# Gated delta rule, second chunk: its gate rows loaded ahead of its keys, with the gates' load ahead of the inverse; banks of the gate rows' filler emptied earlier; last tile's sum and bank copy exchanged

## The chip, the cores and the metric

The kernel runs on one core of a Trainium2 chip. The metric is the device time of one execution in microseconds; the median of three runs is compared.

## What is computed

One step of a recurrent decoder with three token mixers, over 1024 prompt tokens and 8 x 4 sample tokens (1056 columns in all), D_MODEL 1024, four heads of 128, float32. Cut to what matters here:

```python
def mixer(xn, p, st):
    proj = jnp.einsum('btd,dc->btc', xn, p['w_in'])
    ...
    conv = jax.nn.silu(sum(buf[:, j:j + t_len] * cw[j] for j in range(CONV_W)))
    cq, ck, cv = jnp.split(conv, 3, axis=-1)
    beta = jax.nn.sigmoid(gd_b)
    logg = -jnp.exp(p['gd_A_log']) * jax.nn.softplus(gd_a + p['gd_dt_bias'])
    o_gd, S1_gd = gdn_scan(l2n(heads(cq)) * HEAD_DIM ** -0.5, l2n(heads(ck)), heads(cv), beta, logg, S0_gd)
    y_gd = unheads(head_rms(o_gd) * p['gd_norm_w']) * jax.nn.silu(gd_z)
    ...

# gdn_scan, one chunk
    G = jnp.cumsum(gc, -1)
    decay = jnp.exp(jnp.where(incl, G[..., :, None] - G[..., None, :], -jnp.inf))
    A = eye + jnp.where(strict, bc[..., :, None] * kk * decay, 0.0)
    sol = lax.linalg.triangular_solve(A, rhs, left_side=True, lower=True, unit_diagonal=True)
    ...

# behind the mixers
    x = x + mix
    hid = jnp.square(jax.nn.relu(rmsnorm(x, p['norm2_w']) @ p['w_up']))
    x = x + hid @ p['w_down']
    # and a last rmsnorm of x
```

## The kernel before, in words

Every weight product (`dense`, L432) is made in three products of a high and a low part of weights and activations: a tile of 128 output rows by 1056 columns is three groups of 352 columns, each a chain of 24 matmuls in one of two PSUM banks `D`. A group can start when its bank was emptied by ScalarE (`evac_proj` at L451, for the tiles of the convolution `evac_conv` at L507 to L511 into `u_in`). For each weight tile SyncE (SP) loads `w_raw` (512 KB), ScalarE makes `w_hi` (L406) and GpSimd (POOL) makes `w_lo` (L412). A stored tile goes out by a DMA that ScalarE issues (L458, `proj<-stage`); it counts on `stage_stored`.

Each engine runs its own program in order; semaphores join them. The small steps of a mixer stand between pieces of weight tiles: at each `slot()`, a `Filler` puts the next few pieces (thirds of a group) of its tiles on PE, and on ScalarE and POOL the work that belongs to them. How many pieces a slot takes is a table (`ROW_SLOTS`, `GD_SLOTS`). On ScalarE a bank copy of a slot is kept back until the next slot (`late`), save where a slot has over four pieces, or `slot.evacuate()` is called.

Three places matter here.

1. **Gate rows** (`rows`, from 45 to 75 us). The rows of the gates (36 partitions) are loaded, VectorE and ScalarE make running sums, maxima and exponentials of them, and PE turns pieces of them (L1503 to L1512). Beside it PE fills in with tiles 2 and 3.

2. **The delta rule's first chunks** (`gdn`, from 250 us). The eight prompt chunks of 128 tokens follow one another. SP loads for each the keys and queries (`d_qk`), values (`d_v`), four gate rows broadcast over the partitions (`d_bc`), the gates `z` (`d_z`), each 256 KB for one DMA, and from the buffer `td` the diagonal blocks of an inverse (`d_t`, `d_tt`, 16 KB each, eight of them). The inverse was made by POOL and VectorE before, and SP writes it out to `td` (`inverse_loads(3)`, L716). The loads for chunk n + 1 are issued during chunk n, and VectorE and ScalarE prepare that chunk's decay there (`gdn_ahead`, L1569 and L1580). `stored_all` waits until the stores of all tiles below a number have landed; for `GD0` = 17 these are `stage_stored[0]` for tiles 0, 14 and 16 and `stage_stored[1]` for 1 and 15. It guards the load of `d_z` for the first chunk, since the tiles 14 to 16 are the gates.

3. **The last tile** (`last_down`). In the last feed-forward product each group (g, d) of a tile's eight output rows d is added to `acc` by VectorE (L2826), squared by ScalarE (L2821), and the squares are added up by VectorE (L2833). PE sums over the partitions (L2789 and L2790), ScalarE makes the root (L2782, L2784), and VectorE scales (L2794) what SP stores.

Of the kernel before, what the change touches and what calls it, by code (L numbers as in the profile page):

```python
# [9 lines left out]
ALU = mybir.AluOpType  # L10
# [18 lines left out]
KT = D_MODEL // P  # L29
# [68 lines left out]
class Tile:  # L98
# [8 lines left out]
    @property  # L107
    def slot(self):
        return self.base % 2
# [15 lines left out]
def build(nc, xT, w_proj, w_half, w_full, par, con, rowpar, segrow, m0, conv0, st_ml, st_mn, st_gd, st_hg,  # L125
# [6 lines left out]
    with ExitStack() as ctx:  # L132
# [1237 lines left out]
        def rows(kind, eng, slot):  # L1370
# [16 lines left out]
            if kind == "dve":  # L1387
# [39 lines left out]
                slot()  # L1427

# [38 lines left out]
            if kind == "act":  # L1467
                eng.wait_ge(*rw_dve.after("bc"))
# [20 lines left out]
                slot()  # L1489
                eng.wait_ge(*rw_pe.after("tok"))  # L1490
# [6 lines left out]
            if kind == "pool":  # L1497
                for _ in range(4):
                    slot()
            if kind == "pe":  # L1500
                slot()
                eng.wait_ge(*rw_dve.after("loc"))
                eng.transpose(M[1][0:1, 0:RP], r_a[0:RP, 0, last:CH], ident[0:RP, 0:RP])  # L1503
                eng.transpose(M[1][0:1, RP:2 * RP], r_l[0:RP, last:CH], ident[0:RP, 0:RP]).then_inc(*rw_pe.step("ends"))
                slot()
                eng.wait_ge(*rw_dve.after("mp"))
                eng.transpose(M[2][0:RP, 0:1], r_c[0:1, 3 * RP:4 * RP], ident[0:1, 0:1]).then_inc(*rw_pe.step("prev"))
                slot()
                eng.wait_ge(*rw_dve.after("kd2"))
                eng.wait_ge(*rw_act.after("ex2"))  # L1510
                for q in range(5):
                    i = eng.transpose(M[0][:, q * (RP + H):(q + 1) * (RP + H)], r_tok[q], ident[0:RP + H, 0:RP + H])  # L1512
                i.then_inc(*rw_pe.step("tok"))
                slot()
# [83 lines left out]
        def gdn(kind, eng, n, slot, sample, with_next=False, between=None):  # L1598
# [59 lines left out]
            if kind == "sp":  # L1658
# [8 lines left out]
                if between != "rest":  # L1667
                    for k in range(2):
                        eng.dma_start(hn(B.qk, k * C4), pcols(GD_TILE + 4 * (1 - k), 4, col0, N)).then_inc(gx_in if sample else gd_in, 16)
# [12 lines left out]
                eng.dma_start(hn(B.v), pcols(GD_TILE + 8, 4, col0, N)).then_inc(gx_in if sample else gd_in, 16)  # L1682
                if n is not None or sample:
                    prefetch(eng, None if sample else n, (gd_dve, "ge"))
                    token_rows()
# [3 lines left out]

                if sample:  # L1690
                    gates()
                    eng.dma_start(flat_bh(d_Ss), of_state(st_gd)).then_inc(gxs_ld, 16)
                    return
                prefetch(eng, n, (gd_dve, "zs"))
                if n is not None:
                    gates()
                else:
                    inverse_loads(eng, 3)
                    eng.wait_ge(zeroed, 2)
# [6 lines left out]
                if n is None:  # L1706
                    stored_all(eng, GD0)
                    gates()
                else:
                    slot()  # L1710
# [590 lines left out]
        SCALED = {3: (0,), 4: (1, 2), 5: (3, 4), 6: (5, 6), 7: (7,)}  # L2301
# [470 lines left out]
        def last_down(kind, eng):  # L2772
# [27 lines left out]
            for g, d in GROUPS if kind != "pool" else ():  # L2800
# [23 lines left out]
                if kind == "dve":  # L2824
                    eng.wait_ge(groups_done, n + 1)
                    eng.tensor_tensor(acc[:, d, cols(g)], acc[:, d, cols(g)], bank, ALU.add).then_inc(bank_free[n % 2], 1)  # L2826
                    if d:
# [3 lines left out]
                        else:  # L2831
                            eng.wait_ge(*dve_.after(f"a{g}{d - 2}"))
                            eng.tensor_tensor(SUM3[:, cols(g)], SUM3[:, cols(g)], SQ3[(d - 1) % 2][:, cols(g)], ALU.add).then_inc(*dve_.step(f"a{g}{d - 1}"))  # L2833
                    for k in SCALED.get(d, ()) if g else ():
                        scale(g - 1, k)
# [20 lines left out]
        ROW_SLOTS, ML_SLOTS = [9, 2, 4, 3], [3, 3, 3, 3, 3, 3]  # L2856
# [110 lines left out]
        def _(sp):  # L2967
# [61 lines left out]
            chunk_loads(sp, gdn, LOOP_GD, 0, 3)  # L3029
# [255 lines left out]
```

## Time and profile before

| | |
|---|---|
| median of 3 runs | 2195.5 us (2195.11 to 2198.4) |
| the profiled execution | 2200.46 us |
| its span | 2198.7 us |
| busy: PE / VectorE / ScalarE / POOL | 99% / 44% / 34% / 26% |
| mean granted clock of TensorE | 0.995 |

The profiled execution is a run of its own; its time is 1.8 us above its span, which is the time outside of the first and the last instruction. All rows come from it. Times in rows are microseconds from the start of the span, unless marked ns.

### The profile page before, as it was taken

Reading aid. Unit: us, or ns where it says so; the run is one execution under the profiler, and the core shown is the slowest. Engines: PE = TensorE matmul, PEld = TensorE weight load, DVE = VectorE, ACT = ScalarE, POOL = GpSimd, SP = SyncE. Lnnn points to the kernel's source line nnn. Section 1 sums busy time; section 2 is a strip of 40 time slices with the busy share of each in tenths; the row PEclk is TensorE's granted clock in tenths of the full one; section 3 lists DMA queues with packets and bytes.
Section 4 is the critical chain, followed back from the end, with each engine's and each line's share of the span. In section 5 each row is a group of like instructions: output and inputs, shape, how many; then the busy total and the mean of one; then the engine's idle time right before and its main releaser. Section 6 shows DMA issues by size and latency. Waiting matters only on the chain.

```text
span 2198.7 us, 36263 instructions
## 1 busy us (share of the span) xinstructions
PE 2166.3 (99%) x13762; PEld 2104.9 (96%) x13762; DVE 971.9 (44%) x1522; ACT 758.2 (34%) x1342; POOL 571.2 (26%) x375
## 2 busy tenths in 40 slices
PE   7999999999999999999999999999999999999998
PEld 6999999999899999899998999999999999999997
DVE  5888323333665664244445365442222222222225
ACT  5556323232465563233332333231312213122132
POOL 2438623323211212212212222212221221212120
PEclk9999999999999999999999999999999999999999
DMA  4224536442244323456431744202111111111112
GB/s 173 67 80 135 162 114 188 128 133 89 83 125 144 99 97 118 128 161 193 143 109 59 254 148 146 97 25 58 29 58 34 52 52 33 57 33 52 52 40 88
DMA packets 191538, 222.09 MB, mean 101 GB/s; under 512 B 38670, under 2 KB 146226, under 8 KB 191334
## 3 DMA queue, kind: packets, MB, share of 16 engines
q1 hardware_dynamic: 164364, 179.81, 27.0%
q10 hardware_dynamic: 27098, 41.23, 5.3%
q8 instruction: 53, 0.87, 0.2%
q14 instruction: 23, 0.19, 0.0%
HBM read 162.22 MB, written 58.77 MB: 101 GB/s over the span
## 4 chain that ended last, share of the span: by engine, by line
PE 79%; issue 8%; POOL 4%; DVE 4%; DMA 2%; ACT 2%; SPq 1%; ACTq 0%; POOLq 0%; DVEq 0%
PE D L432 65%; PE D L2811 2%; POOL w_lo L412 2%; POOL b_t L738 1%; POOL b_u L735 1%; DVE u_x L546 1%; PE MM L1302 1%; PE MM L1890 1%; DMA proj<-stage 0%; PE MM L2367 0%; PE MB L1974 0%; PE MM L872 0%; PE MB L2284 0%; PE D L2367 0%; PE MB L2234 0%
## 5 line engine op out<-in xcount | busy, mean ns | idle before, releaser
L432 PE MATMUL D<-xn_hi,w_hi 128*128 128x352 f32 x1992 | 663.7, 333 | 7.3 <-ACT stage L451 2.8
L412 POOL TENSOR_TENSOR w_lo<-w_raw,w_hi 128x1024 fp32r<-128x1024 f32 (+1 forms) x163 | 338.7, 2078 | 1184.7 <-ACT w_hi L406 1184.7
L432 PE MATMUL D<-xn_lo,w_hi 128*128 128x352 f32 x1992 | 644.2, 323 | 0.0
L432 PE MATMUL D<-xn_hi,w_lo 128*128 128x352 f32 x1992 | 643.9, 323 | 0.0
L432 PEld LDWEIGHTS D<-xn_hi,w_hi 128*128 128x128 f32 x1992 | 375.7, 189 | 22.5 <-issue 12.8
L432 PEld LDWEIGHTS D<-xn_lo,w_hi 128*128 128x128 f32 x1992 | 375.8, 189 | 4.7 <-issue 3.8
L432 PEld LDWEIGHTS D<-xn_hi,w_lo 128*128 128x128 f32 x1992 | 375.5, 189 | 0.0
L406 ACT ACTIVATE w_hi<-w_raw 128x1024 fp32r<-128x1024 f32 (+1 forms) x163 | 143.7, 882 | 346.8 <-PE D L432 296.4
L432 PE MATMUL D<-z_lo,w_hi 128*128 128x352 f32 x768 | 247.9, 323 | 0.0
L432 PE MATMUL D<-z_hi,w_lo 128*128 128x352 f32 x768 | 247.8, 323 | 0.0
L432 PE MATMUL D<-z_hi,w_hi 128*128 128x352 f32 x768 | 247.2, 322 | 0.0
L432 PE MATMUL D<-h_lo,w_hi 128*128 128x352 f32 x672 | 217.1, 323 | 0.0
L432 PE MATMUL D<-h_hi,w_lo 128*128 128x352 f32 x672 | 216.6, 322 | 0.0
L432 PE MATMUL D<-h_hi,w_hi 128*128 128x352 f32 x672 | 216.5, 322 | 0.0
L2748 DVE TENSOR_TENSOR acc<-acc,D 128x352 f32<-128x352 f32 x168 | 87.5, 521 | 225.0 <-PE D L432 225.0
L451 ACT ACTIVATE stage<-D 128x352 f32<-128x352 f32 x177 | 80.8, 457 | 239.8 <-PE D L432 223.5
L432 PEld LDWEIGHTS D<-z_hi,w_hi 128*128 128x128 f32 x768 | 144.2, 188 | 0.1
L432 PEld LDWEIGHTS D<-z_hi,w_lo 128*128 128x128 f32 x768 | 144.3, 188 | 0.0
L432 PEld LDWEIGHTS D<-z_lo,w_hi 128*128 128x128 f32 x768 | 144.2, 188 | 0.1
L2734 ACT ACTIVATE f_v<-f_u 128x352 f32<-128x352 f32 x96 | 47.8, 498 | 246.2 <-DVE f_u L2741 246.2
L432 PEld LDWEIGHTS D<-h_hi,w_hi 128*128 128x128 f32 x672 | 126.3, 188 | 0.0
L432 PEld LDWEIGHTS D<-h_hi,w_lo 128*128 128x128 f32 x672 | 126.2, 188 | 0.0
(557 smaller groups left out, 3066.6 us busy)
## 6 DMA issues: line engine op xcount, KB each, us to landing
w_raw<-in_w_proj SPq DMA_DIRECT2D x73, 512.0 KB, 3.7
proj<-stage ACTq DMA_DIRECT2D x60, 528.0 KB, 3.3
w_raw<-in_w_half SPq DMA_DIRECT2D x72, 256.0 KB, 2.7
w_raw<-in_w_full SPq DMA_DIRECT2D x24, 512.0 KB, 3.6
stage<-proj SPq DMA_DIRECT2D x23, 528.0 KB, 3.6
d_bc<-rowd SPq DMA_DIRECT2D x32, 256.0 KB, 5.7
m_in<-proj SPq DMA_DIRECT2D x32, 256.0 KB, 3.8
f_w<-in_w_full SPq DMA_DIRECT2D x16, 512.0 KB, 3.5
```

The source lines that it names most:

```text
L406: nc.scalar.activation(w_hi[t.slot][:, 0:kt, :], buf[:, 0:kt * P].rearrange("p (k m) -> p k m", m=P), ACT.Copy).then_inc(w_hi_made, 1)
L412: nc.gpsimd.tensor_tensor(w_lo[t.slot][:, 0:kt, :], raw(t)[0][:, 0:kt * P].rearrange("p (k m) -> p k m", m=P), w_hi[t.slot][:, 0:kt, :].bi ...
L432: last = nc.tensor.matmul(D[b][:, 0:GN], w[t.slot][:, k, :], x, start=(k == 0 and n == 0), stop=(k == kt - 1 and n == 2))
L451: nc.scalar.activation(stage[:, t.slot, g * GN:(g + 1) * GN], D[t.bank(g)][:, 0:GN], ACT.Copy).then_inc(bank_free[t.bank(g)], 1)
L546: eng.scalar_tensor_tensor(x, conv_in(c)[:, j + 1:j + 1 + CONV_LEN], tap(j + 1), x, ALU.mult, ALU.add).then_inc(*cv_dve.step(f"{now}{c}"))
L735: pool.tensor_tensor(part, b_a[:, k + 1:BLK, k:k + 1].to_broadcast([P, n, k + 1]), b_t[:, k, 0:k + 1].unsqueeze(1).to_broadcast([P, n, k + ...
L738: pool.tensor_tensor(b_t[:, k + 1:BLK, 0:k + 1], b_t[:, k + 1:BLK, 0:k + 1], part, ALU.subtract).then_inc(*iv_pool.step(f"t{k}"))
L1302: i = eng.matmul(level(j, slice(0, N))[:, h * (N // 2):(h + 1) * (N // 2)], hn(g_kl, j * N4)[:, h, :], g_ql[:, j * HF + h * (N // 2):j * H ...
L1890: i = eng.matmul(MM[0:N, h * 2 * N:(h + 1) * 2 * N].rearrange("p (x n) -> p x n", n=N), hn(B.qk, C4)[:, h, :], q_and_k, start=True, stop=True)
L2734: eng.activation(v, u, ACT.Square).then_inc(f_sq, 1)
L2748: eng.tensor_tensor(acc[:, m - FT, cols], acc[:, m - FT, cols], D[t.bank(g)][:, 0:GN], ALU.add).then_inc(bank_free[t.bank(g)], 1)
L2811: last = eng.matmul(bank, w[:, k, :], x[:, k, cols(g)], start=(k == 0 and j == 0), stop=(k == FT - 1 and j == 2))
```

## The change

Four edits. In `rows`, the first slot of nine pieces is split in three and six, every engine gets one more slot, and ScalarE calls `slot.evacuate()` in two places. In `gdn` for SP, a new mode `ahead` issues only the waits and the four `d_bc` loads of the next chunk, and `behind` the rest; the second chunk's loads (n = 0) are taken out of the loop and written with them. In the same function, for the first chunk, `stored_all` and the load of `d_z` are placed ahead of `inverse_loads(3)`, where they stood behind the loads of `d_t` and `d_tt`. In `last_down`, for the last of the eight rows, VectorE's sum of squares stands ahead of the addition to `acc`, and the scaling of one piece goes from the seventh to the eighth step.

```diff
@@ rows, ScalarE and PE
             if kind == "act":
+                slot()
+                slot.evacuate()
                 eng.wait_ge(*rw_dve.after("bc"))
...
                 slot()
+                slot.evacuate()
                 eng.wait_ge(*rw_pe.after("tok"))
...
             if kind == "pe":
+                slot()
                 slot()
                 eng.wait_ge(*rw_dve.after("loc"))
@@ gdn, SP
                 if between != "rest":
-                    for k in range(2):
-                        eng.dma_start(hn(B.qk, k * C4), ...)
+                    if between != "ahead":
+                        for k in range(2):
+                            eng.dma_start(hn(B.qk, k * C4), ...)
...
-                eng.dma_start(hn(B.v), pcols(GD_TILE + 8, 4, col0, N))...
-                if n is not None or sample:
+                if between != "ahead":
+                    eng.dma_start(hn(B.v), pcols(GD_TILE + 8, 4, col0, N))...
+                if (n is not None or sample) and between != "behind":
                     prefetch(eng, None if sample else n, (gd_dve, "ge"))
                     token_rows()
...
+                if between == "ahead":
+                    return
...
                 if n is not None:
                     gates()
                 else:
+                    stored_all(eng, GD0)
+                    gates()
                     inverse_loads(eng, 3)
                     eng.wait_ge(zeroed, 2)
...
-                if n is None:
-                    stored_all(eng, GD0)
-                    gates()
-                else:
+                if n is not None:
                     slot()
@@ last_down, VectorE
-                    eng.wait_ge(groups_done, n + 1)
-                    eng.tensor_tensor(acc[:, d, cols(g)], acc[:, d, cols(g)], bank, ALU.add)...
+                    def gather():
+                        eng.wait_ge(groups_done, n + 1)
+                        eng.tensor_tensor(acc[:, d, cols(g)], acc[:, d, cols(g)], bank, ALU.add)...
+
+                    if d < KT - 1:
+                        gather()
                     if d:
...
+                    if d == KT - 1:
+                        gather()
@@ tables and the SP program
-        SCALED = {3: (0,), 4: (1, 2), 5: (3, 4), 6: (5, 6), 7: (7,)}
+        SCALED = {3: (0,), 4: (1, 2), 5: (3, 4), 6: (5,), 7: (6, 7)}
-        ROW_SLOTS, ML_SLOTS = [9, 2, 4, 3], [3, 3, 3, 3, 3, 3]
+        ROW_SLOTS, ML_SLOTS = [3, 6, 2, 4, 3], [3, 3, 3, 3, 3, 3]
...
-            chunk_loads(sp, gdn, LOOP_GD, 0, 3)
+            gdn("sp", sp, 0, None, False, between="ahead")
+            load_w(sp, Tile(LOOP_GD + 2), w_proj[LOOP_GD + 2])
+            gdn("sp", sp, 0, lambda: load_w(sp, Tile(LOOP_GD + 3), w_proj[LOOP_GD + 3]), False, between="behind")
+            chunk_loads(sp, gdn, LOOP_GD, 1, 3)
```

SP's queue around the first chunk, before: the rest of the first chunk's loads (from `d_v`) and the loop's first turn up to its first load. In a row stand the line, what the DMA writes and reads, its shape, and the semaphores that it waits for.

```order
50 L1682 DMA d_v<-proj 128x4x128 [waits cv_st0,rw_mo,cv_st1,rw_out,rw_dve,rw_act,rw_pe]
51 L716 DMA td<-b_t 128x1024 [waits iv_pool]
52 L716 DMA td<-b_tt 128x1024 [waits iv_dve]
53 L1705 DMA d_t<-td 32x4x32 [waits iv_st,zeroed]
54 L1705 DMA d_t<-td 32x4x32 x3
55 L1705 DMA d_tt<-td 32x4x32 [waits iv_stt]
56 L1705 DMA d_tt<-td 32x4x32 x3
57 L1688 DMA d_z<-proj 128x4x128 [waits stage_stored1,stage_stored0]
```

And now:

```order
50 L1689 DMA d_v<-proj 128x4x128 [waits cv_st0,rw_mo,cv_st1,rw_out,rw_dve,rw_act,rw_pe]
51 L1695 DMA d_z<-proj 128x4x128 [waits stage_stored1,stage_stored0]
52 L716 DMA td<-b_t 128x1024 [waits iv_pool]
53 L716 DMA td<-b_tt 128x1024 [waits iv_dve]
54 L1716 DMA d_t<-td 32x4x32 [waits iv_st,zeroed]
55 L1716 DMA d_t<-td 32x4x32 x3
56 L1716 DMA d_tt<-td 32x4x32 [waits iv_stt]
57 L1716 DMA d_tt<-td 32x4x32 x3
58 L1680 DMA d_bc<-rowd 128x4x128 [waits gd_dve,gd_pool,gd_pe]
59 L1680 DMA d_bc<-rowd 128x4x128 x3
60 L384 DMA w_raw<-in_w_proj 128x1024 [waits w_lo_made]
61 L1675 DMA d_qk<-proj 128x4x128 [waits gd_pool,gd_pe]
```

`d_z` with its wait for the stores went from behind the reads of the inverse to ahead of its writes; the four `d_bc` loads of the second chunk come before weight tile 19 and the keys.

ScalarE in the gate rows, before (`rw_dve`, `rw_act`, `rw_pe` count the steps of the rows, `groups_done` the groups of PE):

```order
53 L1469 ACTIVATE r_row<-r_a 36x256 [waits rw_dve]
54 L1471 ACTIVATE r_a<-r_row 36x256 [waits rw_act]
...
58 L1477 ACTIVATE r_row<-r_a 36x128 [waits rw_act]
59 L406 ACTIVATE w_hi<-w_raw 128x1024 [waits w_loaded1,groups_done]
60 L507 ACTIVATE u_in<-D 128x352 [waits groups_done] x2
...
69 L406 ACTIVATE w_hi<-w_raw 128x1024 [waits w_loaded0,groups_done]
70 L1493 ACTIVATE tok<-MB 128x4x8 [waits rw_pe]
71 L1493 ACTIVATE tok<-MB 128x4x8 x4
72 L1495 ACTIVATE tok<-MB 32x5x4
73 L507 ACTIVATE u_in<-D 128x352 [waits groups_done] x2
```

And now:

```order
53 L406 ACTIVATE w_hi<-w_raw 128x1024 [waits w_loaded1,groups_done]
54 L507 ACTIVATE u_in<-D 128x352 [waits groups_done]
55 L1472 ACTIVATE r_row<-r_a 36x256 [waits rw_dve]
...
60 L1480 ACTIVATE r_row<-r_a 36x128 [waits rw_act]
61 L507 ACTIVATE u_in<-D 128x352 [waits groups_done]
...
70 L406 ACTIVATE w_hi<-w_raw 128x1024 [waits w_loaded0,groups_done]
71 L507 ACTIVATE u_in<-D 128x352 [waits groups_done] x2
72 L1497 ACTIVATE tok<-MB 128x4x8 [waits rw_pe]
```

`w_hi` of tile 3 and the first bank copy of tile 2 went ahead of the first exponential, and two bank copies of tile 3 ahead of the `tok` copies.

## Rows read from the trace of the kernel before

**Rows 1.** The page, busy time of PE: us (share of the span) and instructions.

```profile
PE 2166.3 (99%) x13762; PEld 2104.9 (96%) x13762; DVE 971.9 (44%) x1522; ACT 758.2 (34%) x1342; POOL 571.2 (26%) x375
```

**Rows 2.** The waits of PE over the whole span: us in total, times, longest.

```profile
PE D L432 <- ACT stage L451: 2.8, 1, 2.8
PE D L432 <- ACT u_in L507: 2.4, 2, 1.6
...
PE MM L2789 <- ACT f_q L2821: 1.3, 1, 1.3
```

**Rows 3.** Timeline of PE: start, duration, engine, line, operation [idle before and releaser].

```profile
59.48 0.43 PE L432 MATMUL D<-xn_hi,w_hi 128*128 128x352 f32 x1 [0.81 <-ACT u_in L507]
...
73.97 0.43 PE L432 MATMUL D<-xn_hi,w_hi 128*128 128x352 f32 x1 [1.62 <-ACT u_in L507]
...
273.12 0.66 PE L432 MATMUL D<-xn_hi,w_hi 128*128 128x352 f32 x1 [2.84 <-ACT stage L451]
```

**Rows 4.** Timeline of ScalarE in the gate rows.

```profile
56.29 0.42 ACT L1469 ACTIVATE r_row<-r_a 36x256 f32<-36x256 f32 x1 [5.67 <-DVE r_a L1392]
...
58.04 1.04 ACT L406 ACTIVATE w_hi<-w_raw 128x1024 fp32r<-128x1024 f32 x1
...
72.01 1.06 ACT L406 ACTIVATE w_hi<-w_raw 128x1024 fp32r<-128x1024 f32 x1 [1.32 <-PE D L432]
...
73.43 0.84 ACT L507 ACTIVATE u_in<-D 128x352 f32<-128x352 f32 x2
```

**Rows 5.** Timeline of VectorE in the gate rows.

```profile
63.85 0.21 DVE L1392 TENSOR_SCALAR r_c<-MB 1x64 f32<-1x64 f32 x1 [1.26 <-PE MB L1504]
```

**Rows 6.** Timeline of SP's queue: start, time to issue, line, DMA, how many.

```profile
249.40 0.34 SPq L716 DMA_DIRECT2D td<-b_t  x1
251.56 0.34 SPq L716 DMA_DIRECT2D td<-b_tt  x1
252.12 2.49 SPq L1705 DMA_DIRECT2D d_t<-td  x4
254.70 1.81 SPq L1705 DMA_DIRECT2D d_tt<-td  x4
256.62 0.39 SPq L1688 DMA_DIRECT2D d_z<-proj  x1
...
259.94 4.00 SPq L1674 DMA_DIRECT2D d_bc<-rowd  x4
```

**Rows 7.** Timeline of ScalarE's queue, the store of tile 16.

```profile
250.59 0.34 ACTq L458 DMA_DIRECT2D proj<-stage  x1
```

**Rows 8.** DMA issues from 249 to 253 (last number: us to landing); landing of `d_tt`.

```profile
proj<-stage ACTq DMA_DIRECT2D x1, 528.0 KB, 2.8
td<-b_t SPq DMA_DIRECT2D x1, 512.0 KB, 2.7
td<-b_tt SPq DMA_DIRECT2D x1, 512.0 KB, 3.1
...
DMA to landing us min/median/max: 1.7/1.7/1.8
```

**Rows 9.** The tile `d_bc` from 259 to 272: who waited, and landings.

```profile
  DVE d_de L1569: 4.6, 1
...
DMA to landing us min/median/max: 5.0/5.7/7.4
```

**Rows 10.** Stretches: length, busy PE, PEld, DVE, ACT, POOL, granted clock, DMA share, GB/s.

```profile
271.60:278.60 7.00, 5.48 (x20) 5.48 (x21) 0.82 (x2) 1.81 (x6) 0.93 (x1) 0.52 0.47 158
278.60:285.60 7.00, 7.00 (x54) 7.00 (x54) 1.38 (x2) 2.50 (x4) 2.37 (x1) 1.00 0.14 44
```

**Rows 11.** Timeline of PE, the product that reads `d_t`.

```profile
257.91 1.15 PE L1949 MATMUL MB<-d_t,d_mt 128*128 128x128 f32 x8
```

**Rows 12.** Timeline of VectorE and ScalarE at the last bank copy.

```profile
2188.01 0.52 DVE L2826 TENSOR_TENSOR acc<-acc,D 128x352 f32<-128x352 f32 x1
...
2188.63 0.50 ACT L2821 ACTIVATE f_q<-acc 128x352 f32<-128x352 f32 x1 [1.41 <-DVE acc L2826]
```

More of the change, by code:

```diff
@@ L1497, in rows @@
             if kind == "pool":
-                for _ in range(4):
+                for _ in range(5):
                     slot()
             if kind == "pe":
+                slot()
                 slot()
@@ L1667, in gdn @@
                 if between != "rest":
-                    for k in range(2):
-                        eng.dma_start(hn(B.qk, k * C4), pcols(GD_TILE + 4 * (1 - k), 4, col0, N)).then_inc(gx_in if sample else gd_in, 16)
+                    if between != "ahead":
+                        for k in range(2):
+                            eng.dma_start(hn(B.qk, k * C4), pcols(GD_TILE + 4 * (1 - k), 4, col0, N)).then_inc(gx_in if sample else gd_in, 16)
                 def token_rows():
@@ L1681, in gdn @@
                         eng.wait_ge(s_, 16 * NCONV // 2)
-                eng.dma_start(hn(B.v), pcols(GD_TILE + 8, 4, col0, N)).then_inc(gx_in if sample else gd_in, 16)
-                if n is not None or sample:
+                if between != "ahead":
+                    eng.dma_start(hn(B.v), pcols(GD_TILE + 8, 4, col0, N)).then_inc(gx_in if sample else gd_in, 16)
+                if (n is not None or sample) and between != "behind":
                     prefetch(eng, None if sample else n, (gd_dve, "ge"))
@@ L2824, in last_down @@
                 if kind == "dve":
-                    eng.wait_ge(groups_done, n + 1)
-                    eng.tensor_tensor(acc[:, d, cols(g)], acc[:, d, cols(g)], bank, ALU.add).then_inc(bank_free[n % 2], 1)
+                    def gather():
+                        eng.wait_ge(groups_done, n + 1)
+                        eng.tensor_tensor(acc[:, d, cols(g)], acc[:, d, cols(g)], bank, ALU.add).then_inc(bank_free[n % 2], 1)
+                    if d < KT - 1:
+                        gather()
                     if d:
```

## Prediction

> **What bounds the kernel now.** I read the page first, then the waits, then the places of the waits in the timeline. TensorE is busy for 99% of the span [rows 1], so no other engine's busy time matters: the kernel ends earlier only by what is taken out of TensorE's gaps, or by clock that it gets back. The span is 2198.7 us and PE is busy for 2166.3 of it: all gaps together are 32.4 us. Most lie in the first 51 us and after the last product, where the change touches little. The list of PE's waits [rows 2] names those that it can reach: 2.8 us for `stage` (one wait), 2.4 us for `u_in` (two) and 1.3 us for `f_q` (one). The timeline puts them at 273.12, at 59.48 and 73.97 [rows 3], and at the end.
>
> The wait of 2.84 us at 273.12 costs more than itself. In the 7.0 us from 271.6 to 278.6 the granted clock was 0.52, so the lower of the two levels (1.2 GHz, of 2.4), after TensorE had stood idle from about 270.3; in the next 7.0 us it was 1.00 [rows 10]. PE was busy 5.48 us in the slow stretch, so it gave away half of that, 2.74 us. The two waits for `u_in` (0.81 and 1.62 us) cost nothing besides themselves.
>
> **Gate rows.** ScalarE is the engine to watch. In `rows` it emptied D banks only after the exponentials: the chain starts at 56.29, after a wait of 5.67 us, `w_hi` of tile 3 follows at 58.04, and only then come the two `u_in` copies [rows 4], so PE stood 0.81 us for a bank. Now `w_hi` and the first `u_in` stand ahead of the exponentials. PE's wait began at 58.67, with tile 2's second group done. The first was done one group of 24 products earlier; at the 54 instructions in 7.00 us of [rows 10], 0.13 us each and rather more for these wide ones, that is 55.5 or sooner. So the copy fits into the idle 5.67 us and PE's wait goes: 0.81 us. VectorE then gets `ends` sooner too, since it waited 1.26 us for PE there [rows 5], so the chain behind it moves along rather than swallowing the gain. In the second place `w_hi` of tile 4 starts at 72.01 and runs 1.06 us, and the `u_in` copies come at 73.43, behind six small `tok` copies [rows 4]; the new order lets them start when `w_hi` is done, near 73.0: 0.45 us. Together **-1.3 us**. From both sides: 0 if the chain holds ScalarE all the same, -2.4 if both waits vanish. I take -1.3, nearest the rows. Added slots on DVE issue nothing; POOL's order of instructions stays.
>
> **Rows ahead of keys.** The four `d_bc` loads of the second chunk are issued from 259.94 for 4.00 us, behind a weight tile (512 KB) and keys, queries and values (three of 256 KB) [rows 6]. VectorE stood 4.6 us for them, and they took 5.0 to 7.4 us to landing [rows 9]; ScalarE waits for VectorE there with the bank copies queued behind, which is PE's 2.84 us. Moved ahead of those 1.25 MB they follow the `d_tt` reads directly. That takes this wait away, and its clock: **-2.84 - 2.74 = -5.6 us**. What is late next: weight tile 19 and keys, now behind the rows. The tile is wanted by ScalarE some 20 us later and POOL's product with the keys has nothing behind it until then, so I cost both at nothing.
>
> **The gates' load moves too, and that is the price.** On SP the wait for both `stage_stored` counters stood behind the first chunk's `d_t` and `d_tt` reads; it now stands ahead of the writes of the inverse (`td`). SP takes its work in order. The store that it waits for is the last tile's (tile 16), issued by ScalarE at 250.59 [rows 7], 2.8 us to landing [rows 8]: 253.4. But the writes of `td` were issued at 249.40 and 251.56, and `d_t` and `d_tt` were read from 252.12 and 254.70 [rows 6], each read waiting for its write to land. PE came to the product that reads them at 257.91 with no wait to see [rows 11], and the last read must have landed right by then: issued near 256.1, 1.7 to landing [rows 8]. There is no slack.
>
> Step by step, in the times of before: store landed 253.4; `d_z` 0.39 and two `td` writes 0.34 each, with small gaps, so `td<-b_t` at 253.9 and `td<-b_tt` at 254.3. The first lands 2.7 to 3.2 us later (it now shares the DMA engines with `d_z` and the second), at 256.6 to 257.1. Four `d_t` reads take 2.49: 259.1 to 259.6. The four `d_tt` took 1.81 to issue; from their start to the last landing were 3.2 us at most before (254.70 to 257.91): 262.3 to 262.8. PE then stands from 257.9, so **+4.4 to +4.9; I take +4.6 us**. The lower bound is 2.8 (store landing in 2.4 us, `d_t` issued in 1.9), the upper 5.6 (each landing half a us longer). PE's work before it shifts by the 1.3 us won above and the store with it, so the two terms add.
>
> A wait of this size is longer than the 2.84 us that brought the clock down, so I expect the lower clock here too, and take the same 2.74 us; if more of the slow stretch falls into the wait itself, about 2.0. **+2.7 us.** With the wait, everything behind it in the chunk is some 7 us later, so the second chunk's rows (issued from about 261.4, 5.0 to 7.4 us to landing [rows 9]) are there before VectorE asks.
>
> The trace prices each link from issue to landing at 1.7 to 3.1 us, of which data take only part. The Trainium skill (DMA: Bandwidth & Descriptors, Anatomy of one DMA) gives every DMA a fixed cost of about 2.0 us that overlaps with nothing when the next waits for it, mostly the confirmation that the write has landed. With its 2.0 us and 1.2 us for 512 KB the link from `td` to `d_t` would be 3.2 us against 2.7 in the trace, and the stall, an estimate, 5.1 instead of 4.6 us. It speaks against putting one more landing ahead of a write and a read that PE waits for; the measured durations are the ones in the sum.
>
> **Last tile.** VectorE's sum at the seventh step goes ahead of its bank copy, and one scaling moves a step later. The copy started at 2188.01, just when PE's last product ended, and the square followed at 2188.63 [rows 12]; PE waited for that square for 1.3 us [rows 2]. The sum (0.52 us) leaves a place behind the copy where only PE's last total needed it, and that total waited for the square, which follows the copy and not the sum. The moved scaling makes the room. So 0; bounds -0.1 (the copy a bit sooner) and +0.5 (the sum delaying it by its whole length). Stores of the output go on behind the final scalings.
>
> **The sum.** -1.3 (gate rows) - 5.6 (rows of the second chunk) + 4.6 (wait for `d_tt`) + 2.7 (clock) + 0 = **+0.4 us**. The profiled execution took 2200.46 us, 5 us more than the median of the three runs (2195.5), so the sum is made as a difference: 2195.9. This kernel's measurement can tell about 0.2%, 4.4 us, from no change.
>
> **The rivals.**
> - *The moved wait costs nothing* (the store has landed, or the inverse comes later than the store). For it: the wait was there before without cost. Against: the store is issued 1.2 us after the first write of `td`, and its landing is 1.8 us after the second [rows 6 to 8]. It gives -1.3 - 5.6 = -6.9, so 2188.6. Halfway, a wait under about 1.6 us without loss of clock gives -5.3. 0.17 for both.
> - *Slower: the wait put in is larger than the one taken out.* Mechanism: SP, the wait for `stage_stored` ahead of `td`. The profiled execution is 5 us longer than the median; if the wait at 273.12 is shorter without the profiler (2.0 us) and leaves the clock alone, then the change takes out 2.0 + 1.3 = 3.3 and puts in up to 5.2 + 2.7 = 7.9: +4.6, so 2200.1. It decides from a wait put in that costs 7.7 us, clock and all. 0.17.
> - *The rows come no sooner*, because they now stand behind the later `d_tt` reads: the 5.6 us stay. But VectorE asks later by the same wait. It gives +6.0 and needs landings of over 8 us. 0.02, among the slower.
> - My own case, the two waits changing places: 0.64, nearly all within 0.2%.
>
> **How the numbers follow.** The own case spans from -1.3 - 5.6 + 2.8 + 2.0 = -2.1 to +0.5 - 5.6 + 5.6 + 2.7 = +3.2: 2193.4 to 2198.7. With half a us to one of spread between runs, and reaching to the others until 2 in 10 are left out: 2189.5 to 2200.5. Faster by over 0.2%: the first rival, 0.17. Slower by over 0.2%: the second and third and a tail, 0.18. Same: 0.65.
>
> **What would show it.** In the new profile: no PE wait at about 59 and a shorter one at about 73; SP issues `d_z` first, then `td`, after 252; a PE wait of 3 to 5 us at the product that reads `d_t` near 257 to 262, named a DMA or not named at all; the lower clock behind it; no wait for `stage` near 272. The sum is wrong if that wait is under 2 us, or if the clock stays at 1.00 behind it, and the case of rows is wrong if `stage` is still waited for.

## The result: 3.9 us slower, and the profile after

The changed kernel took 2200.44 us (median of 17 runs, 2198.75 to 2202.91). The kernel before, run beside it on the same chip, took 2196.51 us (median of 17, 2193.69 to 2201.1). The ratio is 1.0018, with an interval of 1.0012 to 1.0025, so between 2.6 and 5.5 us slower. That is at the edge of what this measurement can tell from no change (0.2%), and on the slow side of it.

The profiled execution of the changed kernel has a span of 2198.6 us, against 2198.7 us in the profile of before. **The two profiles together show no difference, and the medians show 3.9 us.** So the profile of before is one of the longer executions of that kernel (2200.46 us, where its 17 timed runs end at 2201.1), and this matters for everything that was read from it.

The page, busy times, which answer to [rows 1]:

```profile
PE 2162.9 (98%) x13762; PEld 2102.8 (96%) x13762; DVE 969.4 (44%) x1522; ACT 758.2 (34%) x1342; POOL 570.1 (26%) x375
```

The waits of TensorE (PE), changed kernel (what waited, on what; us in total, times, longest), which answer to [rows 2]:

```profile
PE MB L1957 <- DMA d_tt<-td: 5.0, 1, 5.0
...
PE MM L2797 <- ACT f_q L2829: 1.3, 1, 1.3
PE D L432 <- ACT u_in L507: 1.1, 1, 1.1
```

The wait for `stage` (2.8 us) is gone from the list, that for `u_in` fell from 2.4 to 1.1 us, and one of 5.0 us for the reads of the inverse is new. The timeline of PE has them at these places [rows 3, 11]:

```profile
72.10 0.43 PE L432 MATMUL D<-xn_hi,w_hi 128*128 128x352 f32 x1 [1.13 <-ACT u_in L507]
...
261.08 2.07 PE L1957 MATMUL MB<-d_t,d_mt 128*128 128x128 f32 x8 [4.95 <-DMA d_tt<-td]
```

**Gate rows.** The timeline of ScalarE, which answers to [rows 4]:

```profile
54.58 0.47 ACT L507 ACTIVATE u_in<-D 128x352 f32<-128x352 f32 x1 [2.64 <-PE D L432]
56.13 0.42 ACT L1472 ACTIVATE r_row<-r_a 36x256 f32<-36x256 f32 x1 [1.09 <-DVE r_a L1392]
...
70.64 1.06 ACT L406 ACTIVATE w_hi<-w_raw 128x1024 fp32r<-128x1024 f32 x1 [1.32 <-PE D L432]
71.61 0.80 ACT L507 ACTIVATE u_in<-D 128x352 f32<-128x352 f32 x2
```

The bank copy now lies inside ScalarE's idle time, before the exponential at 56.13, and PE has no wait left near 59. The second wait is 1.13 instead of 1.62 us. Tile 2 itself began 0.30 us sooner in this execution (PE at 50.43 against 50.73), so of the 1.87 us by which PE is ahead at this point (72.10 against 73.97) 1.57 us are the edit's. The shorter waits make 1.30 of it; what the other 0.27 us are isn't shown.

**SP's queue around the first chunk**, with the store that it waits for; these answer to [rows 6, 7]:

```profile
248.77 0.34 ACTq L458 DMA_DIRECT2D proj<-stage  x1
...
251.44 0.38 SPq L1695 DMA_DIRECT2D d_z<-proj  x1
251.87 0.50 SPq L716 DMA_DIRECT2D td<-b_t  x1
252.41 0.42 SPq L716 DMA_DIRECT2D td<-b_tt  x1
256.07 1.76 SPq L1716 DMA_DIRECT2D d_t<-td  x4
257.88 1.85 SPq L1716 DMA_DIRECT2D d_tt<-td  x4
259.84 2.04 SPq L1680 DMA_DIRECT2D d_bc<-rowd  x4
```

SP waits for the store issued at 248.77, issues `d_z` at 251.44, and only then the two writes of the inverse. In the profile of before the first write was issued 1.2 us ahead of that store; now it is 3.1 us behind it. The DMA issues of this stretch (last number: us to landing) answer to [rows 8]:

```profile
td<-b_t SPq DMA_DIRECT2D x1, 512.0 KB, 4.1
td<-b_tt SPq DMA_DIRECT2D x1, 512.0 KB, 4.8
d_z<-proj SPq DMA_DIRECT2D x1, 256.0 KB, 3.3
```

The writes land in 4.1 and 4.8 us, where before they took 2.7 and 3.1. PE waits from 256.1 to 261.1. The stretches of the wait and behind it (length, busy PE, PEld, DVE, ACT, POOL, granted clock, DMA share, GB/s) show the clock going to its lower level, as in [rows 10]:

```profile
258.50:265.50 7.00, 4.42 (x18) 4.43 (x19) 0.00 (x0) 2.25 (x4) 0.00 (x0) 0.51 0.52 103
265.50:272.50 7.00, 7.00 (x53) 7.00 (x52) 2.46 (x5) 2.27 (x6) 2.37 (x1) 1.00 0.85 262
```

PE was busy 4.42 us at half clock, so 2.2 us went there. With the wait, the moved load and its wait for the stores put in 7.2 us.

**The rows of the second chunk** are waited for by VectorE for 0.37 us, where it was 4.6 us in [rows 9]. Its timeline, before and then in the changed kernel:

```profile
270.71 0.69 DVE L1569 TENSOR_TENSOR d_de<-d_bc,cst 128x512 f32<-128x512 f32 x1 [4.64 <-DMA d_bc<-rowd]
```

```profile
270.55 0.69 DVE L1574 TENSOR_TENSOR d_de<-d_bc,cst 128x512 f32<-128x512 f32 x1 [0.37 <-DMA d_bc<-rowd]
```

So the rows themselves came no sooner: their loads are issued from 259.84 against 259.94 before, and VectorE starts on them at 270.55 against 270.71. Nearly all of the difference lies with VectorE, which was ready for them 4.1 us later (270.18 against 266.07), since PE had been held up by the new wait.

**The last tile.** VectorE and ScalarE at the last bank copy, which answer to [rows 12]:

```profile
2187.45 0.52 DVE L2845 TENSOR_TENSOR f_sum<-f_sum,f_q 128x352 f32<-128x352 f32 x1
2187.99 0.52 DVE L2835 TENSOR_TENSOR acc<-acc,D 128x352 f32<-128x352 f32 x1
2188.60 0.50 ACT L2829 ACTIVATE f_q<-acc 128x352 f32<-128x352 f32 x1 [1.41 <-DVE acc L2835]
```

The sum moved ahead of the copy; the copy starts at 2187.99 (2188.01 before) and the square waits 1.41 us as before. The exchange is free and brings nothing.

### The profile page after: what moved, and what is told of

Read it like the earlier page. It is cut to its first block, busy times and chain, and to the rows that moved or that the text cites. A ratio compares the mean times of both kernels' runs of the same rounds, so it can differ in the third digit from the quotient of the medians.

```text
span 2198.6 us, 36222 instructions
## 1 busy us (share of the span) xinstructions
PE 2162.9 (98%) x13762; PEld 2102.8 (96%) x13762; DVE 969.4 (44%) x1522; ACT 758.2 (34%) x1342; POOL 570.1 (26%) x375
## 4 chain that ended last, share of the span: by engine, by line
PE 91%; DVE 3%; ACT 3%; DMA 2%; issue 1%; SPq 0%; POOL 0%; ACTq 0%; DVEq 0%
PE D L432 75%; PE MM L1302 2%; PE D L2819 2%; PE MM L872 1%; PE MM L1898 1%; PE MB L1296 0%; DVE u_x L546 0%; DMA proj<-stage 0%; ACT g_lf L935 0%; PE MM L1342 0%; ACT g_lg L1154 0%; PE MB L1957 0%; PE MB L1982 0%; PE MM L1347 0%; PE MB L2292 0%
```

## The experiments

The puzzle: by the profiles the change takes out 2.84 us of wait with 2.74 us of clock, and 1.3 us in the gate rows, and puts in 7.2 us. That nearly cancels, and the two spans agree with it, yet the medians say that the kernel is 3.9 us slower. Either the wait that was taken out is shorter in ordinary executions, or another part costs something that the profile doesn't show. The parts were therefore taken apart. Times are medians (of 6 runs for store_only, 8 for before_again, 10 for wait_alone, 11 for the other experiments). Ratios are against the kernel before on the same chip. It took 2196.51 us (17 runs) beside the full change, 2196.45 us (28) beside store_back, store_only, gate_rows_only and last_tile_only, 2196.55 us (33) beside the next four, and 2197.93 us (15) beside rows_ahead_only. The ratio is not exactly that of the two medians, and can differ from it by up to 0.05%, 1 us.

| kernel | median us | ratio and interval |
|---|---|---|
| full change | 2200.44 | 1.0018 (1.0012 to 1.0025) |
| store_back | 2194.61 | 0.9989 (0.998 to 0.9998) |
| store_only | 2203.11 | 1.0029 (1.0017 to 1.0041) |
| gate_rows_only | 2194.08 | 0.9993 (0.9984 to 1.0002) |
| last_tile_only | 2196.83 | 1.0003 (0.9994 to 1.0012) |
| rows_landed_first | 2194.55 | 0.9988 (0.9979 to 0.9997) |
| writes_then_wait | 2194.12 | 0.9988 (0.9979 to 0.9997) |
| wait_alone | 2199.41 | 1.0008 (0.9998 to 1.0017) |
| before_again | 2196.5 | 0.9998 (0.9988 to 1.0008) |
| rows_ahead_only | 2195.95 | 0.9993 (0.9984 to 1.0002) |

### store_back: the change without the moved wait

```diff
@@ gdn, SP, against the changed kernel
                 else:
-                    stored_all(eng, GD0)
-                    gates()
                     inverse_loads(eng, 3)
...
+                if n is None:
+                    stored_all(eng, GD0)
+                    gates()
-                if n is not None:
+                else:
```

> The full change with one edit undone: the wait for the stores and the load of d_z go back behind the reads of d_t and d_tt. Theory A (the moved wait is the whole loss: 4.95 us of standing plus about 2.2 us of half clock): 7 us less than the changed kernel, 2193.3 us, ratio to before 0.9985, no wait of PE at the product that reads d_t, clock 1.00 there. Theory B (the product waits for something that comes late anyway, the inverse or VectorE): within 1 us of the changed kernel, 2200. If the wait for the rows cost 5.6 us in the timed runs of before too, it would be 2189.5 (ratio 0.997).

Measured: 2194.61 us, 5.8 below the changed kernel and 1.8 below the kernel before; the interval excludes 1 and does not meet that of the changed kernel. The wait at the product that reads `d_t` is gone and the clock is 1.00 there. So the whole loss of the change hangs on the place of the wait for the stores and of the load of `d_z` behind it. But what the other parts gain is 1.8 us, not 6.9; the 2189.5 us that a real gain of 5.6 us would have given did not come. In its profile VectorE still waits for the rows, and a short wait for `stage` is left (timelines of SP, VectorE and PE):

```profile
255.71 2.09 SPq L1680 DMA_DIRECT2D d_bc<-rowd  x4
...
266.94 0.69 DVE L1574 TENSOR_TENSOR d_de<-d_bc,cst 128x512 f32<-128x512 f32 x1 [2.21 <-DMA d_bc<-rowd]
...
269.35 0.43 PE L432 MATMUL D<-xn_hi,w_hi 128*128 128x352 f32 x1 [0.43 <-ACT stage L451]
```

### store_only: nothing but the moved wait

```diff
@@ gdn, SP, against the kernel before
                 else:
+                    stored_all(eng, GD0)
+                    gates()
                     inverse_loads(eng, 3)
...
-                if n is None:
-                    stored_all(eng, GD0)
-                    gates()
-                else:
+                if n is not None:
```

> The kernel before with only the wait for the stores and the load of d_z moved ahead of the inverse's writes. Theory A: +7.1 us from the wait for d_tt and its clock, less whatever the wait for the second chunk's rows cost in timed runs (VectorE asks for them 7 us later, while SP issues them about 4 us later, so most of that wait goes): between 2198 and 2203.6. Theory B: 2196.5, no wait at the product. In its profile: a wait of PE of 4.5 to 5.5 us for d_tt.

Measured: 2203.11 us, 6.7 above the kernel before. Its PE timeline:

```profile
262.89 2.07 PE L1948 MATMUL MB<-d_t,d_mt 128*128 128x128 f32 x8 [4.90 <-DMA d_tt<-td]
```

The stretches of it and behind it (columns as above):

```profile
260.00:267.00 7.00, 4.11 (x16) 4.12 (x17) 0.00 (x0) 1.94 (x4) 0.00 (x0) 0.57 0.64 181
267.00:274.00 7.00, 7.00 (x51) 7.00 (x50) 2.46 (x5) 1.96 (x4) 3.46 (x2) 0.94 0.66 181
```

The wait for `stage` is gone here although the rows were not moved: VectorE was ready for them 6.2 us later (272.29 against 266.07), while they were issued only 4.5 us later (264.48 against 259.94) and took 5.8 us at most to land instead of 7.4, so its wait shrinks to 0.47 us. The moved wait alone does what the rows' move was for, at a higher price. The sum is 4.90 of wait and 2.5 of clock (half of 4.11, and 0.4 in the next stretch). Against 6.7 us measured, the wait that it took out is worth 0.7 us (4.90 + 2.5 - 6.7). The interval of the ratio, 3.7 to 9.0 us, is wide, but a wait worth 5.6 us would leave 1.8 us, which lies outside of it.

### gate_rows_only and last_tile_only: the two other parts

The first has the extra slots, the two `evacuate` calls and the table of the change, and nothing else of it; the second has `SCALED` and `gather` alone.

```diff
@@ gate_rows_only, against the kernel before
             if kind == "act":
+                slot()
+                slot.evacuate()
...
-        ROW_SLOTS, ML_SLOTS = [9, 2, 4, 3], ...
+        ROW_SLOTS, ML_SLOTS = [3, 6, 2, 4, 3], ...
@@ last_tile_only, against the kernel before
-        SCALED = {3: (0,), 4: (1, 2), 5: (3, 4), 6: (5, 6), 7: (7,)}
+        SCALED = {3: (0,), 4: (1, 2), 5: (3, 4), 6: (5,), 7: (6, 7)}
...
+                    if d < KT - 1:
+                        gather()
```

> The kernel before with only the edit of the gate rows (slots of three and six, banks emptied early). Expected by my step: -1.3 to -1.6 us, 2195.0, ratio 0.9993; PE's waits for u_in fall from 2.4 to 1.1 us. Rival (the gain is swallowed by the inverse on POOL, which follows the rows): 0, and a new wait of PE for d_vb or the inverse near 255. Its profile is also another draw of the wait for the second chunk's rows, untouched here: 2.84 us with clock lost if the profile of before is typical, well under that if it was a long one.

> The kernel before with only the edit of the last tile. Expected by my step: 0 (within 0.3 us), PE's wait for f_q stays 1.3 us. Rival (the edit brings the 4 us that the timed runs show and the profiles don't): +4 us. Its profile is a third draw of the wait for the second chunk's rows.

Measured: the gate rows gave -2.4 us by the medians and -1.5 by the ratio (interval -3.5 to +0.4), with 1.1 us of waits for `u_in` left, as in the full change. The last tile gave +0.4 by the medians (-1.3 to +2.6), so nothing that can be told. More telling is a place that neither edit touches, the wait for `stage` in the second chunk. PE's timeline of gate_rows_only:

```profile
269.65 0.43 PE L432 MATMUL D<-xn_hi,w_hi 128*128 128x352 f32 x1 [0.78 <-ACT stage L451]
```

The 7 us around it (columns as above):

```profile
269.00:276.00 7.00, 6.35 (x43) 6.35 (x44) 1.01 (x2) 2.85 (x6) 1.19 (x2) 1.00 0.56 164
```

PE's timeline of last_tile_only:

```profile
271.49 0.43 PE L432 MATMUL D<-xn_hi,w_hi 128*128 128x352 f32 x1 [0.87 <-ACT stage L451]
```

The same wait that took 2.84 us in the profile of before takes 0.8 to 0.9 us here, and the clock stays at 1.00. That pointed at the profiled execution of before, and not at the change.

### before_again: the kernel before, once more

No edit but a comment; the same program, timed and profiled once more.

> The kernel before once more, for another draw of the wait for the second chunk's rows. If the profile of before was a long draw: PE's wait for stage near 270 is 0.5 to 1.2 us, clock 1.00 behind it, and 2194 to 2198 us. If it was typical: 2.5 us or more and the clock at the lower level behind it.

Measured: 2196.5 us. Its wait for `stage`, in PE's timeline:

```profile
272.93 0.43 PE L432 MATMUL D<-xn_hi,w_hi 128*128 128x352 f32 x1 [0.85 <-ACT stage L451]
```

The 7 us around it:

```profile
272.00:279.00 7.00, 6.15 (x42) 6.08 (x42) 1.05 (x2) 3.12 (x7) 1.19 (x2) 1.00 0.52 164
```

VectorE waited 2.8 us for the rows here, and 4.6 us in [rows 9]; the slowest of the four loads took 5.9 us to land here, and 7.4 there. Three profiles of this place as it was before show 0.78, 0.85 and 0.87 us at full clock, and one shows 2.84 us at the lower clock. So the 5.6 us read from [rows 2, 10] come from the one profile of four in which a load landed late. How often that happens in timed runs isn't known; store_only and rows_ahead_only say that it isn't the usual case.

The same profile has the lower clock in another place. Behind the second wait for `u_in`, as long as in [rows 3], PE ran part of the next 7 us at the lower level:

```profile
74.14 0.43 PE L432 MATMUL D<-xn_hi,w_hi 128*128 128x352 f32 x1 [1.62 <-ACT u_in L507]
...
74.14:81.14 7.00, 7.00 (x34) 7.00 (x35) 5.18 (x4) 1.60 (x4) 3.92 (x3) 0.76 0.37 58
```

That is 1.7 us (7.00 at 0.76), which the same wait did not cost in the first profile.

### rows_ahead_only: nothing but the rows' move

```diff
@@ gdn, SP, against the kernel before
-                    for k in range(2):
-                        eng.dma_start(hn(B.qk, k * C4), ...)
+                    if between != "ahead":
+                        for k in range(2):
+                            eng.dma_start(hn(B.qk, k * C4), ...)
...
+                if between == "ahead":
+                    return
@@ the SP program
-            chunk_loads(sp, gdn, LOOP_GD, 0, 3)
+            gdn("sp", sp, 0, None, False, between="ahead")
+            load_w(sp, Tile(LOOP_GD + 2), w_proj[LOOP_GD + 2])
+            gdn("sp", sp, 0, lambda: load_w(...), False, between="behind")
+            chunk_loads(sp, gdn, LOOP_GD, 1, 3)
```

> The kernel before with only the second chunk's d_bc loads ahead of weight tile 19, keys and values; gate rows, last tile and the wait for the stores as before. Three profiles without the edit show PE's wait for stage at 0.78 to 0.87 us with the clock at 1.00, one at 2.84 us with clock lost. Theory E (the edit takes out the typical wait, in part): wait for stage 0.2 to 0.6 us, 2196.5 less 0.3 to 0.8 us, so 2195.7 to 2196.2, which five rounds can hardly tell from no change. Theory F (the profile of before was typical of the timed runs, and the edit is worth 5.6 us): 2190.9, ratio 0.9975.

Measured: ratio 0.9993, so -1.5 us with an interval of -3.5 to +0.4 (-2.0 by the medians); a gain of 5.6 us is refuted. PE has no wait for `stage` in this profile at all, where 0.2 to 0.6 us were expected, so the move alone does take it out. VectorE's timeline:

```profile
268.05 0.69 DVE L1569 TENSOR_TENSOR d_de<-d_bc,cst 128x512 f32<-128x512 f32 x1 [1.52 <-DMA d_bc<-rowd]
```

The landings, from the view of the tile `d_bc` from 250 to 272, which answer to [rows 9]:

```profile
DMA to landing us min/median/max: 4.6/5.6/9.0
```

### rows_landed_first: are the rows slow because of what follows them?

In store_back the rows are issued 2.9 us sooner than in gate_rows_only (255.71 against 258.60), yet VectorE's step on them starts only 0.3 us sooner (266.94 against 267.25). This kernel is store_back, and holds the next weight tile back until the rows have landed.

```diff
@@ the SP program, against store_back
             gdn("sp", sp, 0, None, False, between="ahead")
+            sp.wait_ge(gd_rows, 64 * 2)
             load_w(sp, Tile(LOOP_GD + 2), w_proj[LOOP_GD + 2])
```

> store_back with one more wait: SP holds weight tile 19, keys, queries and values until the second chunk's four d_bc loads have landed. Theory C (those loads share the DMA engines with what is issued right behind them, and so landed as late as 9.6 us after their issue in store_back): d_bc lands within 4.5 us of its last issue, before 262.5; VectorE waits for it no more, PE's wait for stage (0.43 us) goes; 2193.5 to 2194.6 us. Theory D (the broadcast loads are slow by themselves): d_bc lands near 266 as in store_back, PE's wait for stage stays at 0.4 to 0.9 us, same time. Either way keys and tile come about 5 us later, in time for 280.

Measured: 2194.55 us, not to be told from store_back. SP's queue in the timeline:

```profile
256.04 2.09 SPq L1680 DMA_DIRECT2D d_bc<-rowd  x4
264.12 0.35 SPq L384 DMA_DIRECT2D w_raw<-in_w_proj  x1
```

The landings of `d_bc`, from the view of the tile:

```profile
DMA to landing us min/median/max: 4.7/5.5/6.5
```

A mixed answer. With nothing issued behind them the slowest load takes 6.5 us instead of 9.6 in store_back, VectorE has no wait for the rows and starts on them at 264.87 instead of 266.94, and PE's last 0.43 us of wait is gone. From their first issue to the point where they are waited out it is 8.1 us here (256.04 to 264.12, the issue of the tile behind them), 8.7 in gate_rows_only (258.60 to 267.25) and 11.2 in store_back (255.71 to 266.94). So the loads issued behind them are what used up most of the lead of 2.9 us. But 8.1 us of the 11.2 remain with nothing behind, where the first expectation had at most 6.5 (landed before 262.5), and the second had no change. Neither had the size right.

### wait_alone: is it the wait, or `d_z` ahead of the writes?

```diff
@@ gdn, SP, against the changed kernel
                     stored_all(eng, GD0)
-                    gates()
                     inverse_loads(eng, 3)
...
+                if n is None:
+                    gates()
-                if n is not None:
+                else:
```

> The changed kernel with only the wait for the stores ahead of the inverse's writes; d_z is loaded behind d_t and d_tt as before. Theory A (the wait on the landing of the store is the price, d_z's own issue and traffic a small part): PE's wait for d_tt 4.0 to 4.7 us, clock lost, 2199.5 to 2200.4. Rival (d_z's 256 KB on the DMA engines are the price): under 2 us of wait, 2195 to 2196.

Measured: 2199.41 us, +2.9 by the medians (ratio 1.0008; the interval of -0.4 to +3.7 reaches 0). PE's wait fell below what was expected, 3.10 us instead of 4.0 or more, in its timeline; the rows of SP's queue stand below it:

```profile
259.47 2.07 PE L1958 MATMUL MB<-d_t,d_mt 128*128 128x128 f32 x8 [3.10 <-DMA d_tt<-td]
...
251.66 0.34 SPq L716 DMA_DIRECT2D td<-b_t  x1
252.06 0.42 SPq L716 DMA_DIRECT2D td<-b_tt  x1
254.37 1.79 SPq L1715 DMA_DIRECT2D d_t<-td  x4
```

The first write goes out only 0.2 us sooner than in the changed kernel, but it lands 2.7 us after its issue instead of 4.2 (start of the `d_t` reads less start of the write, in both queues). One load of 256 KB ahead of the writes cost 1.85 of the 4.95 us. The waiting itself cost the rest, so neither expectation had the split right. The clock still went down:

```profile
259.00:266.00 7.00, 6.53 (x27) 6.54 (x27) 0.43 (x1) 3.67 (x6) 0.96 (x1) 0.53 0.78 198
```

With the wait shorter, more of the slow stretch falls on work of PE: 6.53 us at 0.53 cost 3.1 us, against 2.2 in the changed kernel. Wait and clock together are 6.2 us here and 7.2 there, and the medians are 1.0 us apart, though the intervals overlap. So by the profiles only about 1 us of the 1.85 us is left in the time.

### writes_then_wait: the writes first

```diff
@@ gdn, SP, against the changed kernel
-                    stored_all(eng, GD0)
-                    gates()
                     inverse_loads(eng, 3)
+                    stored_all(eng, GD0)
+                    gates()
```

> The changed kernel with the two td writes ahead of the wait for the stores, and d_z behind that wait but ahead of the reads of d_t and d_tt. Theory A says that the loss lies in the writes' late start, since their landing then runs while SP waits for the store: the writes are issued near 248.0 and 250.2, and the store has landed by the time td has. PE's wait at the product that reads d_t falls from 4.95 us to 0.5 us (d_z's issue), the clock stays 1.00, and the time is within 1 us of store_back's 2194.6. Rival (the reads of d_t and d_tt are what is slow under d_z's load): 2 us or more of wait remain, with the clock lost, 2198 or more.

Measured: 2194.12 us, 6.3 below the changed kernel and 2.4 below the one before (ratio 0.9988, 0.9979 to 0.9997). SP's queue, and then PE's timeline:

```profile
247.97 0.34 SPq L716 DMA_DIRECT2D td<-b_t  x1
...
251.93 0.39 SPq L1695 DMA_DIRECT2D d_z<-proj  x1
```

```profile
257.61 1.15 PE L1957 MATMUL MB<-d_t,d_mt 128*128 128x128 f32 x8 [1.14 <-DMA d_tt<-td]
```

The 7 us around it:

```profile
256.00:263.00 7.00, 5.86 (x46) 5.67 (x45) 1.49 (x4) 3.68 (x6) 1.97 (x3) 1.00 0.64 144
```

The wait for the stores still stands ahead of the reads, yet it costs PE 1.14 us (0.5 expected) and no clock. The first write goes out at 247.97, ahead of the store (249.11), and has landed while SP waits for it until 251.93, so the landings run beside each other and not one behind the other. This and store_back beat the changed kernel clearly, and the kernel before by intervals that just leave out 1; they can't be told from one another, nor clearly from the gate rows alone.

## Why the prediction held, and where it was 3.5 us off

The forecast was +0.4 us, so 2195.9 us, with 2189.5 to 2200.5 around it. Measured were +3.9 us and 2200.44 us; the kernel before came out 1.0 us above the three runs that the forecast started from, which is the rest of the distance. That the time lies inside the range, by 0.06 us, is luck: the prediction's own case ended at 2198.7. The likeliest case ("the two waits changing places") is what the traces show, but the result stands where the second rival had put it (2200.1), and for that rival's reason. By its steps:

- **Gate rows, -1.3 us: right.** The waits fell from 2.43 to 1.13 us, the second by 0.49 where 0.45 was forecast; the edit is worth 1.6 us by the timeline, and 2.4 by the medians or 1.5 by the ratio, both with a wide interval. The statement that the copy would fit at "55.5 or sooner" holds: it started at 54.58. That these waits "cost nothing besides themselves" is true of the profile that it was read from and not of every execution: in before_again the one of 1.62 us was followed by the lower clock, for 1.7 us. None of the six profiles with the edit, where that wait is 1.13 us at most, has this.
- **Wait put in, +4.6 us: right in size (4.95), by links that were off both ways.** The store landed in 2.7 us (2.8 forecast). The writes were given 2.7 to 3.2 us to land and took 4.1 and 4.8. The load of `d_z` ahead of them makes most of this: in wait_alone, with the two writes 0.4 us apart and nothing right ahead, they took 2.6 and 3.6. The four `d_t` reads were given 2.49 us to be issued and took 1.76; why they took longer before isn't shown. By the figures of the Trainium skill (DMA: Bandwidth & Descriptors, Anatomy of one DMA) the prediction's estimate for this wait was 5.1 us; the trace has 4.95. The nearness is chance as well: with the page's figures a write of 512 KB would take 3.2 us, and here it took 4.1 and 4.8. That section gives them for DMAs that GpSimd issues, and these are SP's.
- **Clock, +2.7 us, or 2.0 with more of the slow stretch inside the wait:** measured 2.2. Right.
- **Rows of the second chunk, -5.6 us: this is the step that failed.** The wait for `stage` is gone, as forecast, but it was worth about 0.85 us and not 5.6: three other profiles have 0.78, 0.85 and 0.87 us, with the clock untouched. store_only and rows_ahead_only say the same from the timed side (0.7 us, and 1.5 with an interval that reaches 0.4 on the other side). Of the mechanism, rows_ahead_only shows that the move by itself takes the wait out. In the changed kernel it did not have to: the rows came no sooner, and VectorE asked 4.1 us later. store_only shows that this alone is enough.
- **Weight tile and keys behind the rows at nothing:** nothing was seen to wait for them in the changed kernel's list of PE's waits. **Last tile, 0:** right, +0.4 us within its interval.
- **The rivals.** The first (the moved wait is free) is refuted by the 4.95 us. The third had its fact right, since the rows came no sooner, and its price wrong: by VectorE asking later, which it names itself, the wait fell to 0.37 us. The second asked for a shorter wait at `stage` in ordinary executions and no clock lost there. That is what three profiles show. Its +4.6 us comes from two sizes that were both too large: it takes out 3.3 us where 2.45 are measured, and puts in 7.9 where 7.2 are. Its chance and that of the third make 0.19 alone, where the prediction gives 0.18 to all that is slower.

With the measured terms: -1.6 (gate rows) - 0.85 (`stage`) + 4.95 + 2.2 = +4.7 us, against +3.9 measured, inside the interval of 2.6 to 5.5. For store_only 4.90 + 2.5 - 0.85 = +6.6 against +6.7. How the failed step came about is plain now. The prediction noted that the profiled execution was 5 us longer than the median, used that to shift the result, and in its own case still took two of its terms (2.84 and 2.74 us) from the very stretch that made it longer: this place was worse by 4.7 us than its usual 0.85.

What stays open is where the rest of the scatter between executions comes from. A large part of it is lower clock in places that no edit touches. As an estimate, PE's busy time times the missing share of the clock, summed over half-microsecond stretches, gives 3.4 us between 1182 and 1197 us in eight of the eleven profiles, 1.7 in two (store_back, last_tile_only) and nothing in gate_rows_only, whose span (2189.5 us) is the shortest. PE has no gap there in any of them: in the 8 us from 1184 it is busy for 8.00 in before, with 0.66 granted, and in gate_rows_only, with 1.00. Another 1.7 us goes in seven profiles between 25 and 30 us, and in three between 891 and 901 us. That makes 1.7 to 6.8 us per profile outside of the places of this change, so single executions say little about a change of 2 us. What starts these stretches is not shown by any run. The timed runs point the same way: the mean granted clock of the kernel before lay between 0.996 (8 of 28 runs, 2198.2 us on average) and 0.999 (one, 2193.45 us), while 14 of 17 runs of the changed kernel were at 0.996.

## What to carry to other kernels

When the profiled execution is clearly longer than the median, look for the part of the trace that makes it so before taking a term from there; one more profile of the unchanged kernel would have shown this wait at 0.85 us instead of 2.84. A wait placed into a queue that works in order costs all landings that it puts one behind the other: keep a write whose landing others wait for ahead of such a wait (writes_then_wait, 1.14 against 4.95 us), and keep other large loads from going out right before it (wait_alone, 3.10 against 4.95 us). A wait's price has to be read together with the clock behind it: the 1.85 us less of wait in wait_alone were about 1 us of time by the profiles. And of two parts that cure the same wait (here the rows' move, and the delay of PE in store_only) only one gains, so a part should be measured without the others.

## What the runs showed of the hardware

- **Landing times of DMAs from 256 KB on depend on their neighbours in the queue, by more than was allowed for.** The same write of 512 KB landed in 2.6 us with a second write 0.4 us behind it (wait_alone), and in 4.1 us with a 256 KB load 0.4 us ahead of it as well (the changed kernel). The broadcast rows, 1 MB in four loads, took 8.1 us from first issue to last landing with nothing behind them and 11.2 us until their reader started with large loads right behind them (store_back), so issuing them 2.9 us sooner brought their reader 0.3 us there.
- **The issue itself gets slower too.** SP's two `d_qk` loads took 0.95 us to issue in gate_rows_only and 3.70 us in the changed kernel, where they follow the broadcast loads. With these landed first it was 1.41 us (rows_landed_first). In the changed kernel:

```profile
261.92 1.31 SPq L384 DMA_DIRECT2D w_raw<-in_w_proj  x1
263.33 3.70 SPq L1675 DMA_DIRECT2D d_qk<-proj  x2
```

- **After the longer waits of PE the clock was always lower, after short ones only sometimes.** All four waits of 2.84, 3.10, 4.90 and 4.95 us were followed by the lower level in the next microseconds, at a price of 2.2 to 3.1 us; those waits cost 1.4 to 2.0 times what the list of waits says. Behind the waits of 0.43 to 1.14 us at `stage` and at the read of `d_t` the granted clock stayed at 1.00. The wait of about 1.6 us for `u_in` near 74 us is in five profiles, and the lower clock followed it in one (before_again, 0.76 in the next 7 us). The waits of 1.3 and 1.7 us near 20 and 24 us are in all eleven, and the lower clock followed them in seven.
